# The last triangular inverses shared between GpSimd and VectorE, and an RWKV scan five steps behind the delta scan

## The reference

```
# delta part, 8 heads of 128, per chunk (k, v, beta, g are of the chunk)
tmat  = inverse(eye + strict_lower(beta * k @ k.T * decay))     # one 64x64 system per chunk, head, direction
v_new = tmat @ (v * beta) - tmat @ (k * beta * exp(g)) @ state
o     = (q * exp(g)) @ state + attn @ v_new                     # attn: masked q @ k.T * decay
state = state * exp(g_last) + k_tail.T @ v_new
# RWKV part, 16 heads of 64, per token
state = state * w_t - (state @ kk_t) b_t.T + v_t k_t.T
o_t   = state @ r_t
```

## Time and profile before

| | us |
|---|---|
| median of three runs | 4449.22 |
| the profiled execution | 4440.76 |
| its span | 4439.1 |
| stage gprep | 2911.8 to about 3133 |
| stage rprep | about 3133 to 3585 |
| stage scan | 3585 to about 4186 |
| of it the 20 loop steps | 3613.9 to about 4126 |

### The profile page before, as it was taken

One profiled execution on the slowest core, in us unless ns is written; L12 is line 12 of the kernel. 1 busy time (PEld: TensorE's weight loads), 2 busy tenths in 40 slices (PEclk: granted clock), 3 DMA queues, 4 the chain that ended last, 5 costly groups with the idle time before them and its releaser, 6 DMA issues. The chain is left out here.

```text
span 4439.1 us, 64109 instructions
## 1 busy us (share of the span) xinstructions
PE 3672.3 (83%) x28116; PEld 2864.8 (65%) x28116; DVE 2147.5 (48%) x2188; ACT 646.0 (15%) x1002; POOL 786.9 (18%) x818
## 2 busy tenths in 40 slices
PE   7499999999997988289999999976467636888793
PEld 1277777777886876168878888854345534677383
DVE  0457787753334542544453343346678834321633
ACT  0022222212000001110110000011133201222001
POOL 0001111111000000025005134000673775000000
PEclk9799999999998999589999999987689767988797
DMA  7355555555343432322233243334458598765222
GB/s 265 106 153 153 151 152 152 152 171 168 103 123 101 141 99 108 107 69 85 77 101 90 80 114 109 111 137 171 126 178 252 158 220 187 187 195 179 72 95 114
DMA packets 666347, 611.49 MB, mean 138 GB/s; under 512 B 150656, under 2 KB 567480, under 8 KB 657760
## 3 DMA queue, kind: packets, MB, share of 16 engines
q1 hardware_dynamic: 567808, 435.15, 34.3%
q0 software_dynamic: 21936, 95.56, 6.6%
q10 hardware_dynamic: 76336, 76.83, 5.3%
HBM read 471.67 MB, written 135.82 MB: 137 GB/s over the span
## 5 line engine op out<-in xcount | busy, mean ns | idle before, releaser
L361 PE MATMUL front_ps<-b_hT,front_wb 128*128 128x512 f32 x4224 | 979.1, 392 | 18.3 <-DVE front_wb L351 18.3
L1251 PE MATMUL in_ps<-b_hT,in_wb 128*128 128x512 f32 (+3 forms) x4992 | 956.4, 353 | 10.7 <-DVE in_wb L1238 10.7
L361 PEld LDWEIGHTS front_ps<-b_hT,front_wb 128*128 128x128 f32 x4224 | 789.7, 188 | 199.0 <-DVE front_wb L351 21.6
L1251 PEld LDWEIGHTS in_ps<-b_hT,in_wb 128*128 128x128 f32 (+1 forms) x4992 | 816.2, 188 | 157.5 <-issue 15.4
L1236 DVE CAST in_wb<-in_raw 128x2048 fp32r<-128x2048 f32 (+1 forms) x68 | 82.6, 1215 | 560.5 <-PE in_ps L1251 543.0
L349 DVE CAST front_wb<-front_raw 128x2048 fp32r<-128x2048 f32 x88 | 108.0, 1228 | 433.8 <-PE front_ps L361 425.1
L755 POOL DMA_DIRECT2D front_mwb<-in_w_ada x128 | 101.7, 798 | 803.6 <-PE front_mps L765 800.9
L351 DVE TENSOR_TENSOR front_wb<-front_raw,front_wb 128x2048 fp32r<-128x2048 f32 x88 | 201.8, 2293 | 3.0
L1003 PE MATMUL merge_ps<-merge_pair,merge_wb 128*128 128x512 f32 x768 | 176.5, 392 | 22.3 <-DVEq L1021 22.3
L1086 PE MATMUL wout_ps<-wout_wb,wout_pair 128*128 128x512 f32 x768 | 176.6, 392 | 15.2 <-DVEq L1107 14.5
L1086 PE MATMUL wo_ps<-wo_wb,wo_pair 128*128 128x512 f32 x768 | 176.8, 392 | 12.9 <-DVEq L1107 12.2
(11 more groups left out here) (420 smaller groups left out, 4715.4 us busy)
## 6 DMA issues: line engine op xcount, KB each, us to landing
front_raw<-in_w_in SPq DMA_DIRECT2D x88, 1024.0 KB, 6.7
in_raw<-in_w_in SPq DMA_DIRECT2D x67, 1024.0 KB, 5.6
front_mwb<-in_w_ada POOLq DMA_DIRECT2D x128, 512.0 KB, 5.1
r_scr<-rprep_ob ACTq DMA_DIRECT2D x16, 2694.0 KB, 13.0
scan_rops<-r_scr SPq DMA_DIRECT2D x24, 1796.0 KB, 11.1
mod_wb<-in_w_ada SPq DMA_DIRECT2D x8, 4096.0 KB, 12.7
g_scr<-gprep_ob SPq DMA_DIRECT2D x8, 3474.0 KB, 11.2
wo_raw<-in_w_o SPq DMA_DIRECT2D x16, 1024.0 KB, 5.0
```

The costliest lines, as they stand in the source:

```text
L361: last = self.nc.tensor.matmul(self.ps[:, n % 2, :], self.wb[:, n % 2, x, kt, :], self.hT[:, y, kt, :], start=kt == term == 0, stop=kt == ...
L1251: last = self.nc.tensor.matmul(self.ps[0:width, n % 3, first:end], self.wb[:, n % 2, x, kt, 0:width], self.hT[:, y, kt, first:end], start= ...
```

## The change

Four things change together.

- **Two engines solve.** GpSimd solves only one of the last two batches (direction 0). The other (direction 1) is solved by VectorE, by the same instructions, in a new class `SideSolver`: SP loads it first of all, VectorE does it in five parts, and ScalarE's queue stores it at step 4. Part 0 (steps 0 to 11 of 31) stands ahead of `g.start`; parts 1 to 4 stand in loop steps 0 to 3, between `g.weigh` and `g.update`. Its room is the first operand buffer of the RWKV scan, so `r.load(sp, 0)` moves from SP's start to loop step 3, behind the wait for the store of VectorE's batch.
- **`LAG` is 5.** Loop step n does RWKV chunk n-5; there are 17 steps. Steps 5 to 8 hold both scans, the RWKV one without outputs; steps 9 to 11 both with outputs; 12 to 16 the RWKV scan alone, with the 8 folds spread over these five steps (two each in steps 12, 13 and 15).
- **The delta operands lie in scan order.** `g_scr` becomes `g_chan[chunk, direction, partition, head, 129]` and `g_tok[chunk, partition, head, 321]`. In gprep a head is stored with three DMAs instead of one, in pieces of 516, 516 and 1284 bytes where they were 2316. In the scan each partition reads one row of 4128 or 10,272 bytes instead of eight pieces of 516 or 1284.
- **SP's start.** The load of VectorE's batch first, then inverse and operands of delta step 0, of step 1, and inverse 2. Before: three inverses, operands of steps 0 and 1, RWKV operands 0.

```diff
     def store(self, sp, i):
         u = i % 2
         sp.wait_ge(self.s["k_out"], i + 1)
-        sp.dma_start(self.g_scr[:, i:i + 1].rearrange("c h p x -> p (c h) x"), self.ob[:, u]).then_inc(self.stored[u], 16)
+        for d in range(2):
+            sp.dma_start(self.g_chan[:, d, :, i, :].rearrange("c p x -> p c x"),
+                         self.ob[:, u, :, G_CH * d:G_CH * (d + 1)]).then_inc(self.stored[u], 16)
+        sp.dma_start(self.g_tok[:, :, i, :].rearrange("c p x -> p c x"), self.ob[:, u, :, 2 * G_CH:G_COLS]).then_inc(self.stored[u], 16)
...
-            rows = self.g_scr[STEPS[k][d]].rearrange("h p x -> p h x")
-            sp.dma_start(self.chan[:, u, d], rows[:, :, G_CH * d:G_CH * (d + 1)]).then_inc(self.loaded[u], 16)
-            sp.dma_start(self.tok[r, u], rows[r, :, 2 * G_CH:G_COLS]).then_inc(self.loaded[u], 16)
+            sp.dma_start(self.chan[:, u, d], self.g_chan[STEPS[k][d], d]).then_inc(self.loaded[u], 16)
+            sp.dma_start(self.tok[r, u], self.g_tok[STEPS[k][d], r]).then_inc(self.loaded[u], 16)
...
+class SideSolver:
+    PARTS = (0, 12, 17, 22, 27, HC - 1)
...
+    def load(self, sp):
+        sp.dma_start(self.rows, self.source).then_inc(self.n_in, 16)
+    def solve(self, dve, link, part):
+        ops = self.nc.vector
+        if part == 0:
+            dve.wait_ge(self.n_in, 16)
+            invert_begin(ops, link, self)
+        invert_steps(ops, link, self, self.d, self.PARTS[part], self.PARTS[part + 1])
+        if part == len(self.PARTS) - 2:
+            invert_end(ops, link, self, self.d)
+            dve.sem_inc(self.solved, 1)
+    def store(self, act_e):
+        act_e.wait_ge(self.solved, 1)
+        act_e.dma_start(self.source, self.rows).then_inc(self.y_out, 16)
-LAG = 8
+LAG = 5
...
-        solver = Solver(st, "sp", r.ops[0:BATCH, 1].rearrange("p d q x -> p (d q x)"))
+        rooms = [r.ops[0:BATCH, u].rearrange("p d q x -> p (d q x)") for u in range(2)]
+        solver = Solver(st, "sp", rooms[1])
+        side = SideSolver(nc, st, systems, 2, 1, rooms[0])
+        tiles_at = lambda n: [t for t in range(GH) if NCH + t * LAG // GH == n]
...
-                for n in range(3):
-                    g.load_inverse(sp, n)
-                for n in range(2):
-                    g.load(sp, n)
-                r.load(sp, 0)
+                side.load(sp)
+                g.load_inverse(sp, 0)
+                g.load(sp, 0)
+                g.load_inverse(sp, 1)
+                g.load(sp, 1)
+                g.load_inverse(sp, 2)
...
                     if n == LAG - 2:
-                        sp.wait_ge(solver.y_out, 32)
+                        sp.wait_ge(side.y_out, 16)
+                        r.load(sp, 0)
+                        sp.wait_ge(solver.y_out, 16)
                         for m in range(3):
                             r.load_inverse(sp, m)
                         r.load(sp, 1)
...
-                    if n >= NCH:
-                        out.fold(pe, n - NCH)
-                    if n > NCH:
-                        out.add(pe, n - NCH - 1)
+                    for t in tiles_at(n):
+                        out.fold(pe, t)
+                        if t > 0:
+                            out.add(pe, t - 1)
...
+                    if n == 4:
+                        side.store(act_e)
...
             def _(dve):
-                g.start(dve)
                 r.start(dve)
                 out.start(dve)
+                side.solve(dve, r.link, 0)
+                g.start(dve)
                 for n in range(NCH + LAG):
                     if in_g(n):
                         g.remainders(dve, n)
                         if in_g(n + 1):
                             g.clear(dve, n + 1)
                         g.weigh(dve, n)
+                    if n < 4:
+                        side.solve(dve, g.link, n + 1)
...
-                for d in range(2):
-                    solve(nc, pool, link, solver, systems, 2, d, d)
+                solve(nc, pool, link, solver, systems, 2, 0, 0)
```

55 lines of the change are left out of this document (33 added, 22 removed).

## The result

The changed kernel takes 4488.16 us (median of 4 runs, 4485.95 to 4496.54) against 4451.16 us (4 runs, 4447.55 to 4461.03): a ratio of 1.008, 95% interval 1.0063 to 1.0096. It is slower by 37 us, where 16 were forecast. The profiled executions differ by 45.1 us of span (4484.2 and 4439.1).

| stretch of the profiled execution | before | after | change | forecast |
|---|---|---|---|---|
| up to the start of gprep | 2911.8 | 2912.9 | +1.1 | 0 |
| gprep | 221.2 | 231.2 | +10.0 | +2 |
| rprep | 451.6 | 453.5 | +1.9 | 0 |
| scan: start of the stage to TensorE's release by the RWKV inverses | 180.6 | 152.0 | -28.6 | -30.3 |
| scan: release to the end of the loop | 357.1 | 417.3 | +60.2 | +44.1 |

What follows compares the result with a forecast made beforehand. The scan was taken as bound by GpSimd's two inverse solves until TensorE's release, then by TensorE. Terms: -30.3 (earlier release) + 44.1 (lag) + 2 (gprep) = +15.8 us, giving 4465 us; range 4437 to 4490.

Steps and rivals of the forecast that it cites:

- my own case: Whole kernel: the summed forecast without any rival, spanning 4453 to 4478 us; chance 0.50.
- the rival of widened holes: Joint scan steps: TensorE's idle gaps grow because five steps load both scans' operands; 31 us more, 4496; chance 0.17.
- Taking turns: Scan start: VectorE and GpSimd solving together delay each other; a VectorE operation grows by most of a GpSimd operation.
- slice 1: VectorE's solve in step 0: 10 operations of some 506 elements beside GpSimd, 15.6 us; undisturbed 7.2.
- Slice 2: VectorE's solve in step 1: 10 operations of some 476 elements, GpSimd at its small last steps, 8.7 us.
- Part 0: VectorE's solve ahead of the delta scan: 24 operations in step with GpSimd, 23.0 us; undisturbed 12.3.
- Slices 3 and 4: VectorE's solve in steps 2 and 3: 5.6 us with GpSimd done, then 5.4 us.
- The rival of undisturbed slices: Scan start: VectorE and GpSimd hardly meet, saving 23 us, 4442; chance 0.20.
- The new stall: Step 4: TensorE waits for loads behind step 3's end, 26 us (20 to 38), and restarts 30.3 us earlier.
- The lag of five steps: Behind TensorE's release: three delta steps now lie beside RWKV steps at 14.7 us each, 44.1 us later; bounds 42 and 52.
- The tail of gprep: End of gprep: the last head's store in short pieces moves at 300 instead of 389 GB/s, 2 us more; bounds 0 and 5.
- a rival in which they close: Steps with RWKV work: emptier DMA queues shrink TensorE's idle time to 2.0 us a step, 36 us off, 4429; chance 0.13.

Runs made afterwards that it cites:

- pool_idle: The changed kernel without the 62 tensor operations of GpSimd's solve in the scan stage (its load, copies and store stay): 4481.28 us, ratio 1.006.
- small_loads: The changed kernel with operand loads of delta steps 5 to 11 and RWKV steps 2 to 11 cut to one of eight heads: 4393.11 us, ratio 0.9865.
- lag5_alone: The kernel before with a lag of 5 and the folds spread, GpSimd alone solving, old layout: 4507.91 us, ratio 1.0122.
- old_layout: The changed kernel with delta operands stored and loaded as in the kernel before; two engines solve, lag 5: 4486.06 us, ratio 1.0065.
- inverse_first: The changed kernel with the first RWKV inverse's load moved in SP's queue ahead of the delta load for step 5: 4483.51 us, ratio 1.0058.
- prefetch_spread_lag9: The kernel before with a buffer per GpSimd batch, RWKV operand loads spread, RWKV inverses ahead of step 7's delta load, lag 9: 4450.51 us, ratio 0.999.

## Why the prediction was right and where it was wrong

The sign and the mechanism held: a solve on two engines that releases TensorE some 30 us earlier, and a lag that puts back more than that. The range held with little to spare: 4488 is 2 us below its upper end, and 10 above the 4478 that I gave as the top of my own case. That top was added up too low: with 38 us of loading and 52 for the lag, the bounds named beside it, it is 4485. The room above was meant for the rival of widened holes. The steps, in their order:

- **Taking turns.** I took 15.6 us for slice 1; it took 14.9 and 7.1 without GpSimd (7.2 in my text). Slice 2 was 11.7 instead of 8.7, since GpSimd's load landed 16.4 us after the stage's start and not 10.6 and its solve ran to 86.6, so it was still at large steps then. Part 0 was 16.6 instead of 23.0 for the same reason: its first operations ran before GpSimd's first. Slices 3 and 4 were 5.5 and 5.1 instead of 5.6 and 5.4. The errors cancel: step 4's first subtraction comes 122.8 us after the stage's start, and 3708.9 in my count was 124.3. The rival of undisturbed slices was wrong, and the 16 us of pool_idle are what it would have been worth, not 23.
- **The new stall.** 26 us behind the end of step 3 were 29 to 30: SP needed from 3728.66 to 3752.3 for the inverses. The release is 28.6 us earlier instead of 30.3. That is close partly by luck: the row of 206 GB/s, which I read as loads to 64 partitions, holds pieces of 516 and 1284 bytes of both delta loads, so it mixes the length of the pieces with the number of partitions.
- **The lag of five steps: the step that failed.** I wrote that a delta step beside RWKV steps costs "what it keeps TensorE busy", 14.7 us, and that is right as far as it goes: 41.1 us for three without the loads. But the 2.6 MB of loads of such a step had no term in my sum. With the loads it is 60.2 instead of 44.1, above my bound of 52; 19 us of it come with them. The lag alone stayed within the bound (49.1), so part of the 19 came only together with the earlier release. By the traces the 11 us between the two are low clock, 115 us against 80, and not holes, and part may be scatter.
- **The tail of gprep.** 10 us instead of 2, bounds 0 and 5. I counted the last head's bytes at a lower rate and called the others covered "by the 25 us of a head". The last two heads are 15.5 us apart, the seventh's stores are not through when the eighth's come (some 1 MB is left), and both weigh on the end.
- **The holes.** I had a rival in which they close, decided by whether they come from full DMA queues; the first half of that is true (68.5 us fall to 17.3 when the loads shrink), but the change fills the queues more behind the release instead of emptying them. What I put forward for it was misread: of the steps in the earlier trace rows step 8 has the lightest loads (92 GB/s, with a hole of 4.1 us) and not step 11 (170 GB/s, 2.0 us). In the rival in which they widen, the steps were like those seen (35 to 38 us); its 31 us on top of mine were twice what came.

**What stays open.** Why the instruction packets start late beside the operand loads. Their transfer is not slowed: it takes 1.1 us in mean in the changed kernel and 1.0 with small loads. Whether they are asked for late or stand in a queue behind the loads, no run tells. Also open is how much of the 11 to 14 us between lag5_alone (406 us behind the release) and the changed kernel and old_layout (417 and 420) is real. The first had stood 79 us before, the others 27 to 31, and the low clock makes the difference; what sets it was not tried.

## What to carry to other kernels

A stall in which transfers run is not empty time. Before you cost the end of a stall at its length, count the bytes that it had hidden and lay them beside the work behind it: here 1.6 to 1.8 us for each MB. Two earlier releases (by 21 and by 18 us) gave no more than 5 to 10 us by the medians. The bytes account for only part of that: 6.9 MB more behind the release are some 12 of the 20 us that came back in inverse_first, and 2.5 MB more are 4 to 5 of the 15 in prefetch_spread_lag9. And when heads are stored at the end of a stage, ask whether the store of the last but one is through when the last begins.

## What the runs showed of the hardware

- TensorE was slowed by loads that it did not wait for: joint steps of 26 us at a granted clock of 1.00 became 34 to 38 us at 0.82 to 0.90. Over half of it are holes (51 of 89 us), the rest the same products at the lower of the two levels (1.2 GHz) more of the time: behind the release it was at that level for 115 us in the changed kernel, mostly in spells of 3 to 10 us, and for 15 us with small loads. The Trainium skill, "SBUF — State Buffer", section "Who interferes with whom", says that DMA never contends with a compute engine. The products' own time agrees (300 and 304 us at full clock); small_loads shows that a kernel can lose 89 us to the loads all the same.
- The holes end with late instruction packets: in the changed kernel all 17 holes above 1.5 us end 1.3 to 1.8 us after a packet of 256 TensorE instructions lands, in the kernel before all 18. With the loads cut to an eighth there are 3 such holes.
- Stores in pieces of 516 bytes to DRAM were slower for their bytes: a packet of 516 bytes took 61 to 70 ns in mean, one of 1032 bytes 57, one of 2316 bytes 99. The end of gprep took 22.4 us instead of 14.8 and 13.8, in part for a backlog. The Trainium skill, "DMA: Bandwidth & Descriptors", section "Specifications", has 512 bytes as the least for line rate, on which I had leant beside my sum; the measurement decides, and here 516 bytes were not enough.
- VectorE's 510-element operation with two inputs in SBUF took 1.48 us beside GpSimd and 0.69 without it.
